# A first recurrent head between projection blocks: key taps as TensorE products with diagonals, states and output steps between parts of the following blocks

## What is computed

```python
u = x @ w_in
m_qk, m_v, m_o, m_gates, a_q, a_k, a_v = jnp.split(u, cuts, axis=-1)
qk = jax.nn.silu(_centred_dwconv(qk, conv_w, conv_b))      # 5 taps over the tokens, each channel by itself
q, k = jnp.split(qk, 2, axis=-1)
h_fwd = _mlstm_scan(q, k, vh, g[0], jax.nn.log_sigmoid(g[2]))
h_bwd = flip(_mlstm_scan(flip(q), flip(k), flip(vh), flip(g[1]), flip(jax.nn.log_sigmoid(g[3]))))
h = h_fwd + h_bwd                                          # normed per head, times sigmoid(o), then @ w_out
```

## Time and profile before

| | |
|---|---|
| median of 3 runs | 3517.61 us (3515.96 to 3518.24) |
| time of the profiled execution | 3518.09 us |
| its span in the trace | 3516.3 us |
| TensorE (PE) busy | 3384.4 us, 96% of the span |
| VectorE (DVE) busy | 1766.4 us, 50% |
| ScalarE (ACT) busy | 757.1 us, 22% |
| GpSimd (POOL) busy | 1220.3 us, 35% |
| mean granted TensorE clock | 0.989 of full speed |

### The profile page before, as it was taken

How to read it: one execution, slowest core, us unless ns; L and a number is a source line. 1 busy time by engine, 2 the same in 40 slices (tenths; PEclk the granted TensorE clock), 3 DMA queues, 4 the chain that set the end, 5 groups by cost and what they waited for, 6 DMA issues and landing times.

```text
span 3516.3 us, 40431 instructions
## 1 busy us (share of the span) xinstructions
PE 3384.4 (96%) x16204; PEld 2702.8 (77%) x16204; DVE 1766.4 (50%) x2045; ACT 757.1 (22%) x1140; POOL 1220.3 (35%) x534
## 2 busy tenths in 40 slices
PE   7999999999999999989999999999999999999997
PEld 6777877778888888867886668888888876767775
DVE  5344544463333333488765653223223357988835
ACT  4233100030000000242224440000000023144352
POOL 2212334434444444332331133333434432432322
PEclk9999999999999999999999999999999999999998
DMA  2101211111111111121211111111111110111111
GB/s 98 46 31 45 90 48 48 48 36 48 48 48 48 50 51 48 36 68 54 84 47 34 35 36 48 48 48 48 48 48 48 48 36 31 53 41 41 41 36 66
DMA packets 47294, 171.80 MB, mean 49 GB/s; under 512 B 5472, under 2 KB 6112, under 8 KB 47200
## 3 DMA queue, kind: packets, MB, share of 16 engines
q1 hardware_dynamic: 38016, 138.43, 12.0%
q10 hardware_dynamic: 9184, 32.03, 2.6%
HBM read 165.71 MB, written 4.72 MB: 48 GB/s over the span
## 4 chain that ended last, share of the span: by engine, by line
PE 86%; DVE 7%; issue 3%; ACT 3%; POOL 1%; DMA 0%; ACTq 0%; DVEq 0%; POOLq 0%
PE acc L396 70%; PE acc L414 4%; PE acc L838 2%; PE acc L814 2%; PE acc L433 1%; DVE conv_slots L1986 1%; PE acc L483 1%; PE acc L791 1%; PE acc L803 1%; DVE rstd L701 1%; POOL w_lo L2300 0%; DVE h L998 0%; PE acc L537 0%; DVE band_scores L906 0%; POOL w_hi L2286 0%
## 5 line engine op out<-in xcount | busy, mean ns | idle before, releaser
L2286 POOL TENSOR_TENSOR w_hi<-raw,zero 128x1024 fp32r<-128x1024 f32 x264 | 517.4, 1960 | 2240.0 <-PE acc L396 1600.2
L396 PE MATMUL acc<-x_hi,w_hi 128*128 128x512 f32 x2512 | 778.7, 391 | 8.0 <-POOL w_lo L2300 2.3
L396 PE MATMUL acc<-x_hi,w_lo 128*128 128x512 f32 x2512 | 774.8, 390 | 0.0
L396 PE MATMUL acc<-x_lo,w_hi 128*128 128x512 f32 x2512 | 774.6, 390 | 0.0
L2300 POOL TENSOR_TENSOR w_lo<-raw,w_hi 128x1024 fp32r<-128x1024 f32 x262 | 696.5, 2658 | 20.5
L998 DVE TENSOR_TENSOR h<-h,acc 128x1024 f32<-128x1024 f32 x320 | 390.3, 1221 | 386.5 <-PE acc L396 384.6
L396 PEld LDWEIGHTS acc<-x_hi,w_hi 128*128 128x128 f32 x2512 | 470.6, 188 | 109.0 <-issue 9.1
L396 PEld LDWEIGHTS acc<-x_lo,w_hi 128*128 128x128 f32 x2512 | 472.4, 188 | 98.7
L396 PEld LDWEIGHTS acc<-x_hi,w_lo 128*128 128x128 f32 x2512 | 472.3, 188 | 98.4
L493 ACT ACTIVATE hid_hi<-hid 128x1024 fp32r<-128x1024 f32 x44 | 46.7, 1061 | 925.7 <-DVE hid L1386 469.7
L1986 DVE SCALAR_TENSOR_TENSOR conv_slots<-conv_slots,par 128x1024 f32<-128x1024 f32 x120 | 227.5, 1896 | 4.1
(11 more groups left out here) (358 smaller groups left out, 3997.4 us busy)
## 6 DMA issues: line engine op xcount, KB each, us to landing
raw<-blocks SPq DMA_DIRECT2D x264, 512.0 KB, 3.3
h<-x_t ACTq DMA_DIRECT2D x8, 512.0 KB, 8.4
h<-x_t ACTq DMA_DIRECT2D x1, 4096.0 KB, 14.0
q_past<-q_dram ACTq DMA_DIRECT2D x8, 512.0 KB, 5.6
w_own<-r_dram ACTq DMA_DIRECT2D x8, 512.0 KB, 6.8
out_t<-out_rows ACTq DMA_DIRECT2D x8, 512.0 KB, 3.0
near_bias<-bias ACTq DMA_DIRECT2D x4, 896.0 KB, 4.6
band_bias<-bias ACTq DMA_DIRECT2D x4, 640.0 KB, 4.0
```

What stands on the lines that cost most here:

```text
L396: ins = pe.matmul(acc[s][:, c], w[:, slot, tile, :], part[:, c], start=(n == 0 and m == 0), stop=(n == last and m == 2))
L2286: pool.tensor_tensor(hi, whole, nothing, ALU.add).then_inc(hi_split, 1)
```

## The change

Three things are done, all around head 0.

1. The keys' five taps are made by TensorE. ScalarE makes five matrices `key_taps`, each the identity times one tap's weights; `first_keys` multiplies them with shifted views of the padded input, 10 float32 matmuls of 512 columns, which sum up in `NUM[1]`. Silu is then applied from there. VectorE's five instructions for the keys go.
2. Head 0's steps are put between parts of blocks: the output gate's block is cut at tile 2, with the keys' and values' transposes between; `carry_states` and `own_scores` stand behind it; the block of head 1's queries is cut at tile 4, `outputs(0)` and `outputs(1)` between; `outputs(2)` stands behind it; the block of head 1's keys is cut at tile 4, with `outputs(3)` between.
3. To match, VectorE's and ScalarE's lists are ordered anew: VectorE makes the states before the masks and decayed queries, and **head 1's queries' taps come behind `h_ready` instead of ahead of the output steps**. ScalarE does the keys' Silu before it issues `ends_all` and `load_rows`, and the columns of the heads behind these.

```diff
+        def first_keys(pe):
+            pe.wait_ge(padded, 1)
+            pe.wait_ge(taps_made, 1)
+            for half in range(2):
+                for j in range(TAPS):
+                    ins = pe.matmul(acc_all[:, 3 * TOK + half * HALF:3 * TOK + (half + 1) * HALF], key_taps[:, j, :],
+                                    conv_in[:, 1, 2 + j + half * HALF:2 + j + (half + 1) * HALF],
+                                    start=(j == 0), stop=(j == TAPS - 1))
+            ins.then_inc(taps_full, 1)
...
         def gates_tensor(pe, t):
...
+            s = claim(pe, t)
+            first_keys(pe)
             pe.wait_ge(rows_done, 3)
-            s = claim(pe, t)
...
         def gates_scalar(act, t, ch):
...
+            for j in range(TAPS):
+                ins = act.activation(key_taps[:, j, :], ident[:, :], ACT.Copy, scale=col("heads", TAPS + 1 + j))
+                ch.link(ins) if j < TAPS - 1 else ins.then_inc(taps_made, 1)
...
+            act.wait_ge(head_ready, 1)
+            act.wait_ge(taps_full, 1)
+            act.activation(conv_out[:, 1, :], NUM[1], ACT.Silu, bias=head_par[:, 2 * TAPS + 1:2 * TAPS + 2])\
+               .then_inc(conv_ready, 1)
             act.wait_ge(r_out, 48)
...
             load_rows(act, 0)
+            s = await_acc(act, t)
...
+            act.wait_ge(chunk_full, 2)
+            act.activation(v_one[:, :, 0:P], NUM[0].rearrange("p (a b) -> p a b", b=P), ACT.Copy).then_inc(v_made, 1)
             act.wait_ge(ends_in, 32)
...
             take_par(dve, ch, t, 0)
             conv_part(dve, ch, pass_input(t), 0)
-            conv_part(dve, ch, pass_input(t), 1)
...
             else:
-                feature_block(pe, t)
+                out_gate = part_block()
+                out_gate(0, 2)
                 turn_keys_and_values()
...
+                out_gate(2, KT)
+                carry_states()
+                pe.wait_ge(conv_ready, t.next("conv_ready"))
+                made = own_scores()
+                first = part_block()
+                first(0, 4)
             pe.wait_ge(past_made, (TT - 1) * (head + 1))
             pe.wait_ge(acc_free[made[0]], made[1])
             outputs(0)
             outputs(1)
-            block_part(pe, t, slot, s, parts[1], parts[2])
+            if head:
+                following(0, 2)
+            else:
+                first(4, KT)
             outputs(2)
-            block_part(pe, t, slot, s, parts[2], parts[3])
+            if head:
+                following(2, 4)
+            else:
+                following = part_block()
+                following(0, 4)
             outputs(3)
-            block_part(pe, t, slot, s, parts[3], parts[4])
+            following(4, KT)
...
             conv_input(act, t, 1)
+            if head == 0:
+                conv_silu(1, 0)
...
+            own_arguments()
...
+            else:
                 pass_acc(t)
+                carry_states()
+                mask_arguments()
+                decay_past_queries()
+                weigh_scores()
+                query_taken = pass_input(t)
...
             dve.tensor_tensor(h_tok[:, :, :], h_tok[:, :, :], stats[:, 36:44].unsqueeze(2).to_broadcast([P, TT, P]),
                               ALU.mult).then_inc(h_ready, 1)
+            if head == 0:
+                take_par(dve, ch, t, 1)
+                conv_part(dve, ch, query_taken, 0)
```

More of the change, by code:

```diff
@@ L1576, in turn_keys_and_values @@
             def turn_keys_and_values():
-                for _ in range(2):
+                for _ in range(2 if head else 1):
                     pe.wait_ge(conv_ready, t.next("conv_ready"))
@@ L1623, in outputs, with part_block @@
                 t.next("num")
-            feature_block(pe, t)
+            def part_block():
+                slot, s = take_block(pe, t), claim(pe, t)
+                take_turn(pe, t)
+                return lambda first, after: block_part(pe, t, slot, s, first, after)
             if head:
+                feature_block(pe, t)
                 mix_rows(pe, t)
@@ L1655, in conv_silu @@
                     act.wait_ge(head_ready, head + 1)
-                act.wait_ge(conv_summed, 2 * head + part + 1)
+                act.wait_ge(conv_summed, 2 * head + part if head else 1)
                 act.activation(conv_out[:, part, :], conv_out[:, part, :], ACT.Silu,
@@ L1743, in head_vector @@
                 ch.link(ins) if way == 0 else ins.then_inc(k_made, 1)
[L1744 to L1757, removed]
-                pass_acc(t)
[L1759 to L1781, removed]
-                pass_acc(t)
+            def own_arguments():
+                dve.wait_ge(r_in, 64 * (head + 1))
+                for way in range(2):
+                    rows = chunks(w_own[:, way, :])
+                    ch.link(dve.tensor_tensor(rows, rows,
+                                              own[:, 8 * way:8 * way + 8].unsqueeze(2).to_broadcast([P, TT, P]), ALU.add))
@@ new lines, in mask_arguments, with decay_past_queries @@
+            def mask_arguments():
+                ch.sync()
+                for way in range(2):
+                    rows = chunks(w_own[:, way, :])
+                    dve.tensor_tensor(rows, rows, masks[:, way, :].unsqueeze(1).to_broadcast([P, TT, P]), ALU.add)\
+                       .then_inc(args_ready, 1)
+            def decay_past_queries():
+                for way in range(2):
+                    dve.wait_ge(q_exp, 2 * head + way + 1)
+                    ch.link(dve.tensor_tensor(q_past[:, way, :], q_past[:, way, :], conv_out[:, 0, :], ALU.mult))
@@ new lines, in carry_states @@
+            def carry_states():
+                for j in range(TT - 1):
+                    dve.wait_ge(past_full, (TT - 1) * head + j + 1)
+                    bank = acc_all[:, 2 * TOK + j % 4 * HALF:2 * TOK + (j % 4 + 1) * HALF]
+                    if j:
+                        dve.wait_ge(past_made, (TT - 1) * head + j)
+                    for way, (n, to) in enumerate(((j, j + 1), (TT - 1 - j, TT - 2 - j))):
+                        new, out = bank[:, way * 256:way * 256 + P + 1], past[:, way, to, 0:P + 1]
+                        if j == 0:
+                            ins = dve.tensor_copy(out, new)
+                        else:
+                            ins = dve.scalar_tensor_tensor(out=out, in0=past[:, way, n, 0:P + 1],
+                                                           scalar=own[:, 32 + 8 * way + n:33 + 8 * way + n], in1=new,
+                                                           op0=ALU.mult, op1=ALU.add)
+                        ch.link(ins) if way == 0 else ins.then_inc(past_made, 1)
+                    ch.sync()
```

56 lines of the change are left out of this document (32 added, 24 removed).

## The result

The changed kernel takes 3523.61 us (3519.42 to 3527.44, 12 runs), the kernel before, run beside it, 3516.24 (3512.95 to 3519.97): ratio 1.0019, 95% interval 1.0012 to 1.0027. It is slower, by 4 to 9.5 us.

What follows compares the result with a forecast made beforehand. TensorE was taken to bound the kernel. From 3518.1 us, -0.4 up to the head's transposes and +10.3 behind made about 3528, less 0.5 for the runs' median: 3527.5; range 3516 to 3532, the forecast's own 3524 to 3531.

Steps and rivals of the forecast that it cites:

- second rival: Hand-over to head 1 as forecast, head 0 better by early load, kept clock or cheaper products: 3519 to 3524; chance 0.20.
- the seam as told: Hand-over from head 0 to head 1: 10.3 us longer, with two TensorE waits behind VectorE's late taps.
- Part 1: Keys' taps on TensorE: products add 8.7 us, cover the 1.48 us wait; ScalarE's five copies cost nothing.
- Part 2: Head 0, keys to states: no wait for decayed keys, perhaps 2 us at the states instead of 5.28.
- Part 3: Head 0's output steps: wait of 5.7 us for weighed scores, low clock about 2, head's transposes at 1610.
- head 0 itself is worth nothing: Head 0: 10 us less waits and clock against 8.7 of products and a new wait of 2 at most.
- Part 4: Seam to head 1: waits of 2.9 and 7.8 us and low clock of 2 make the hand-over 10.3 longer.
- The rival without the lock: GpSimd's splits do not hold VectorE up: 3511 to 3513, no change or faster; chance 0.13.

Runs made afterwards that it cites:

- e4: The kernel before with only the key products on TensorE added, head 0's order kept; ratio 1.0012.
- e8: The changed kernel with 21 small matmuls, results unused, in TensorE's wait for the weighed scores; ratio 1.0014.
- e6: The kernel before, no key products, with head 0's keys and values transposed behind tile 4 of head 1's queries' block; ratio 0.9995, interval holds 1.
- e2: The changed kernel with head 1's queries' taps between VectorE's second and third output step; ratio 1.0006.
- e3: The changed kernel with head 1's queries' block whole and its taps ahead of the output steps, the keys' block cut at tiles 4 and 5; ratio 0.9984.
- e1: The changed kernel with head 1's queries' taps and their Silu back ahead of head 0's output steps; ratio 1.0023.
- e5: e3 with head 1's queries' taps between VectorE's second and third output step and the keys' block cut at tiles 2 and 4; ratio 0.9979 against the kernel before.
- e9: e5 with 17 small matmuls, results unused, in the wait ahead of the head's transposes; ratio 0.9983 against the kernel before.

## Why the prediction was right, point by point

The direction and the mechanism were right; the size was 10 us against 7.9 in the stage and 7 by the ratio. 1.4 more of the distance between 3527.5 and 3523.61 is the median of before, which was 3517.61 in the runs shown and 3516.24 beside the change.

The result lies at an edge. 3523.61 is in the stated range, but just under the forecast's own 3524 to 3531 and inside the second rival's 3519 to 3524, which had a chance of 0.20; and 0.19% is at the 0.2% that the prediction took as the limit of "no change", to which it gave 0.29 against 0.65. What the trace shows lies between the two: the seam as told, and head 0 better because the load of rows landed early, the second rival's first condition.

- *Part 1* held: 1558.17 - 1549.49 = 8.68 us for the products (8.7), no wait at the gates' transposes. The five ScalarE copies took 1.57 us, at 1515.66, in its idle time. e4 says what the products are worth alone: a loss of 6.5 in the stage.
- *Part 2* was mis-sized, to the cautious side. The sum let ScalarE issue its DMAs behind the Silu, from S + 11.3. They went out at 1558.38, S + 8.9, while the table load was still running. So the rows were there at S + 20.0 (1569.52), not S + 22.5, and TensorE had no wait at all at L1617, where I had about 2.
- *Part 3* held: a wait of 5.78 (5.7), for VectorE's weighed scores, with a split on the four instructions ahead of them (8.57 where 4.7 is the undisturbed time: 3.9, against the 3.5 of the sum), a clock of 0.50 behind, which e8 puts at 1.9 (2). T came at S + 64.5 instead of S + 66. So "head 0 itself is worth nothing" was too hard by 1.7: it is worth 2.1.
- *Part 4* held: T to K was 36.08 (36.3), and the path was the one told. VectorE's `mix_lo` ended at T + 14.6 (14.7), the third row of the mix started behind the first addition at T + 25.3 (25.5), and K came 10.8 later (10.8). VectorE's two tap sequences took 8.78 and 8.85, the number read at 1547 in the kernel before. Between these points the sum was not right: the waits were 2.57 and 6.28 (2.9 and 7.8), and the low clock cost 36.08 - 23.6 - 8.85 = 3.6 (2). The sum had missed a low clock behind the first wait (0.58 from 1630 to 1634). The first two rows ended at T + 19.0 instead of 17.7, mostly by it, and the second wait was shorter by as much, since VectorE alone set its end; so this part of the low clock cost nothing.
- The sum has slips that change little: 1573.5, 7.1 and 3.5 make 1584.1 and not 1584.5, 60 records at 0.12 make 7.2 and not 6.9, and the parts of `mix_lo` make T + 14.5.
- The rival without the lock fell: in the changed kernel and the experiments, the eight tap sequences whose four multiply-adds met a whole split took 8.72 to 8.85 (two each here, in e6 and in e8, one each in e2 and e3), those beside none 5.25 (here, e1, e5). The row at 1591.74 that was given for this rival was one of those beside none: the split there was over at 1590.9. The Trainium skill, SBUF — State Buffer, section "Who interferes with whom", has the shared ports as an exclusive lock, held for a whole instruction while the other engine blocks. The trace agrees but for a small overlap: at the seam GpSimd's two instructions ended at 1618.09 and 1621.43, and the two held multiply-adds each 1.1 us behind, where one alone takes 1.28. The seam without its splits was not tried, so how much of its loss is theirs is argued from these rows (3.5 for each tap sequence), not shown.

What the prediction did not ask is why the taps had been moved. e1 answers it: their input comes from a block that the interleaving ends 12.80 us too late. The loss is thus the price of cutting the block of head 1's queries around the output steps, and e3, which does the block whole first, needs neither the late taps nor the wait.

## What to carry to other kernels

When matmul blocks are cut up to cover waits, look at what each block's result feeds: the covered wait here came back as 10 us one hand-over later, because the next head's input was finished late. Cover a wait with the block whose result is wanted soonest, and put work of the other engine where neither its input nor GpSimd's splits make it late. Moving work from an engine that is not waited for (the keys' taps on VectorE) onto the one that bounds is a loss by itself (e4: 6.5 in the stage, ratio 1.0012); it has to unlock an earlier start to pay. Whether the products do so here is not shown: e3, e5 and e9 have them and are 5 to 7.5 us shorter in the stage, but e6 is 4.3 shorter without them, and no run has the order of e3 or e5 without the products.

## What the runs showed of the hardware

ScalarE's queue issued DMAs (`ends_all` at 1558.38, those of `load_rows` from 1559.24 on) while a table load and an activation that stand ahead of them in its list were still running (1558.32 to 1560.73).

The granted clock of a stretch can differ from one execution to the next though the programs order TensorE's work there alike. From 1500 to 1510, with waits of 2 to 3 us for x_lo, it was 1.00 in the kernel before, 0.51 in the changed kernel (the window above), and in the nine experiments 0.50 to 1.00; the kernel before:

```profile
1500.00:1510.00 10.00, 8.62 (x38) 1.00 0.15 52
```

From the end of the first of these waits to S it took 1549.49 - 1499.80 = 49.69 us in the changed kernel and 1543.77 - 1496.84 = 46.93 before. So this is worth about 3 us of the 5.72 by which the changed kernel's profiled execution came late to S. Behind K, where TensorE's list is the same again, it then took 1875.6 us to the end against 1879.8 (and 1872.6 to 1876.2 in the nine experiments), so that 5.7 and 7.9 less 4.2 make the 9.4 between the two spans. That is why spans of single executions (3516.3 and 3525.7) say less here than sums over the stage.
